# One step for both branches of the short block tiles in a sparse-attention loop, and another order around the first gated-linear-attention pair

## The chip, the cores and the metric

The kernel runs on one core of one Trainium2 chip. It is one program for a whole two-block model, launched once. The metric is device time in microseconds (us): the median of several runs of the kernel.

A core has five engines with queues of their own, each of which works strictly down its list: TensorE (PE; its weight loads are shown apart as PEld), VectorE (DVE), ScalarE (ACT), GpSimd (POOL) and SyncE (SP), which here only issues the transfers of weights. They meet through counting semaphores: `wait_ge(sem, n)` holds an engine until `sem` has reached `n`, and `then_inc(sem, 1)` counts an instruction when it is done. PE writes only into the accumulator memory `ps` (8 banks of 512 float32 columns); everything else lies in the on-chip memory, most of it in one large tensor called `arena`.

## The reference, cut to what matters

The change lies in the mixer of the second block, of which this is the core (512 tokens, width 1024):

```python
proj = h @ w_in
q_nsa, kv_nsa, g_nsa, q_gla, k_gla, v_gla, lr_gla, r_gla, g_merge = split_in_proj(proj)
...
o_a = nsa_attention(q_a, k_cmp, v_cmp, kv[2], kv[3], kv[4], kv[5], gates_a)
log_a = log_sigmoid(lr_gla @ gla_gate_w2 + gla_gate_b) / 16
o_b = gla_chunked(q_gla * 64 ** -0.5, k_gla, v_gla, log_a)     # 4 heads, keys of 64, values of 128
o_b = rmsnorm_2(o_b) * silu(r_gla)
gate_a, gate_b = split(sigmoid(g_merge), 2)
merged = gate_a * (o_a @ w_up_nsa) + gate_b * (o_b @ w_up_gla)
x = x + merged @ w_out
```

Inside `nsa_attention` each of 8 heads (64 wide, in 2 key groups) has three branches: compressed blocks, selected blocks, and a window. With 512 tokens and 16 blocks to select out of 8, the selected branch sees every earlier key, and so does the window of 512. Both are thus plain causal attention, with keys of their own (`k_slc`, `k_win`) and values of their own:

```python
p = softmax(mask(q @ k.T))          # causal
out += gate[branch] * (p @ v)       # for branch in (selected, window)
```

## The kernel before, in words

**How products are made.** Each of the large float32 products is three passes over split operands: a weight unit (128 x 1024) arrives in one of four slots of `ring`, ACT writes its upper part into `w_split` (`hi`, L1086), POOL the remainder (`lo`, L1564), and PE then does 8 x 3 matmuls of 512 columns (`unit`, L402 to L404). A split has two slots, so the split of unit n+2 waits for PE to be done with unit n. `ahead(section, k)` on ACT and on POOL is the split of the unit that comes two after (section, k) in that order. So `ahead("nsa_tm", 0)` splits the unit `kv0` and `ahead("nsa_tm", 1)` the unit `kv1`.

**The order of work** is written out by hand, one list for each engine. Nothing is scheduled by a planner; moving a line moves the instruction in that engine's queue.

**The first GLA pair.** Gated linear attention works on two pairs of heads. For pair 0, POOL makes nine products with decays (`decayed`, L1624 and L1625 for seven levels 6, 5, ... 0, each in two halves, then L1618 for the end and the state); its dictionary `between` says before which of the nine a weight split is slipped in. PE takes the scores in five groups (`pair_scores`, L855 and L866), and between these groups it works on parts of the units `kv0` and `kv1`. DVE gathers the scores level by level (`gather_pair`, L2308 and L2319) and between the levels writes the exponents of pair 1 (L1902, L1903, L1908). Then PE transposes keys (`gla_keys`, L874), runs the unit `r0`, makes the chunk states (`gla_states`, L881), half of the unit `k0`, and the outputs of head 0 (`gla_outputs`, L897 and L900). These need the chained states, which DVE writes in `chain_states` (L1938, L1942). `block_inputs(x)` (L2228, 8 small additions each) prepares the inputs of the compressed branch, which PE uses later (L820). `gate_raw(n)` (L2201) takes a finished unit `r0`, `r1`, ... for the output gate of a head.

**The NSA loop.** The selected and window branches of 8 heads run as 32 steps. A step is (p, x, tt): head pair p (one head from each key group), branch x, token tile tt of 128 queries. Tile tt sees tt + 1 blocks of 128 keys. The tiles of a pair come in the order 3, 0, 2, 1, each with both branches, one after the other. For step e:

- PE `nsa_scores`: one matmul for each of the two heads (L994)
- DVE `nsa_stats`: mask the diagonal block (L2389), negated row maximum (L2391)
- ACT `nsa_exps`: one exponential for each head, with its row sum (L1503)
- DVE `nsa_scale`: reciprocal (L2397), one scaling for each head (L2402)
- PE `nsa_transposes`: one transpose for each head and block (L1003)
- ACT `nsa_copies`: the transposed weights back out of `ps` (L1510)
- PE `nsa_values`: one matmul for each head and block (L1017)

Scores and transposes of step e use the banks 2(e % 3) and 2(e % 3) + 1, so scores of step e+2 wait for the copies of step e-1. In iteration e PE does scores(e+2), transposes(e), values(e-1), and then, where a table `GATE_AT` says so, one or three eighths of one of three units of the section `merge` in bank 7 (`gate_chunks`, L402 to L404 again). In iteration e DVE does scale(e), stats(e+2), and after the last step of a pair the additions `nsa_add` (L2411); ACT does copies(e), exps(e+2), and at fixed iterations a split of a `merge` unit or an upper part of a finished output (`outputs_hi`, L1520), whose remainder POOL then writes (L1734).

## Time and profile before

| | us |
|---|---|
| median of 3 runs | 2227.21 (2226.68 to 2233.23) |
| the profiled execution's own time | 2228.96 |
| its span (first to last instruction) | 2227.2 |
| PE busy in the span | 2159.7 (97%) |
| DVE busy | 1044.9 (47%) |
| ACT busy | 853.7 (38%) |
| POOL busy | 1173.3 (53%) |

The profile is of one execution; times in it are from the start of the span. PE is the engine that is busy nearly all the time, and the weight units that it works through make up most of that. A number of busy time alone doesn't say what bounds a stretch: for this one reads where PE sat idle and what ended each idle time. The granted clock is the share of TensorE's full speed that the chip let it have in a stretch: 1.00 is the level of 2.4 GHz, and about 0.5 the level of 1.2 GHz. The stretch of the first GLA pair lies at about 1450 to 1510 us, the NSA loop at about 1589 to 1692 us.

### The profile page before, as it was taken

The numbers are of one execution on the slowest core, as the hardware profiler recorded it, in microseconds if no ns is written. First come the engines' busy times: TensorE is split into PE (matmuls) and PEld (weight loads), VectorE is DVE, ScalarE is ACT, GpSimd is POOL, SyncE is SP. The second block draws the span as 40 slices with busy tenths as digits, with TensorE's granted clock in tenths as the row PEclk, the third lists the DMA queues.
The fourth block names the chain that finished last, engine by engine and source line by source line (L and its number), as shares of the span: only waits on it lengthen the run. The fifth ranks groups of instructions, "written<-read, shape, count | busy, mean of one in ns | idle before, by whom it ended". The sixth has DMA issues, their size and how long they took to land. (4 is left out here: it accounts for less than half of the span.)

```text
span 2227.2 us, 28340 instructions
## 1 busy us (share of the span) xinstructions
PE 2159.7 (97%) x10458; PEld 1775.8 (80%) x10458; DVE 1044.9 (47%) x1507; ACT 853.7 (38%) x1217; POOL 1173.3 (53%) x635
## 2 busy tenths in 40 slices
PE   8999999999999999899999999989989999999997
PEld 6788878888888988788888888768657888888886
DVE  7766774422433047744431436462684335422433
ACT  6565644222323234334322233434664334322222
POOL 5868755554554355435554555573213555554552
PEclk9999999999999999999999999989999999999999
DMA  4112213332332222123332332313201223332331
GB/s 166 58 57 67 65 60 94 101 105 85 95 109 80 85 88 75 56 84 101 95 106 92 95 112 78 125 49 97 74 11 58 95 95 95 95 109 89 95 108 72
DMA packets 52822, 193.30 MB, mean 87 GB/s; under 512 B 6768, under 2 KB 7680, under 8 KB 52480
## 3 DMA queue, kind: packets, MB, share of 16 engines
q1 hardware_dynamic: 50688, 184.95, 26.4%
q10 hardware_dynamic: 2048, 7.19, 0.9%
q8 instruction: 56, 0.92, 0.2%
q14 instruction: 30, 0.25, 0.0%
HBM read 187.92 MB, written 4.19 MB: 86 GB/s over the span
## 5 line engine op out<-in xcount | busy, mean ns | idle before, releaser
L1564 POOL TENSOR_TENSOR w_split<-ring,w_split 128x1024 fp32r<-128x1024 f32 (+3 forms) x327 | 842.7, 2577 | 833.6 <-ACT w_split L1086 833.6
L1086 ACT CAST w_split<-ring 128x1024 fp32r<-128x1024 f32 (+3 forms) x327 | 356.3, 1090 | 1012.2 <-PE ps L404 873.5
L402 PE MATMUL ps<-u_split,w_split 128*128 128x512 f32 x1768 | 706.9, 400 | 18.6 <-DVE u_split L1776 10.9
L404 PE MATMUL ps<-u_split,w_split 128*128 128x512 f32 x1768 | 692.7, 392 | 0.0
L403 PE MATMUL ps<-u_split,w_split 128*128 128x512 f32 x1768 | 692.1, 391 | 0.0
L402 PEld LDWEIGHTS ps<-u_split,w_split 128*128 128x128 f32 x1768 | 334.2, 189 | 96.9 <-issue 22.7
L404 PEld LDWEIGHTS ps<-u_split,w_split 128*128 128x128 f32 x1768 | 334.1, 189 | 71.0
L403 PEld LDWEIGHTS ps<-u_split,w_split 128*128 128x128 f32 x1768 | 334.3, 189 | 69.4 <-issue 3.1
L402 PE MATMUL ps<-hid,w_split 128*128 128x512 f32 x648 | 253.9, 392 | 4.2 <-DVE arena L2061 2.8
L404 PE MATMUL ps<-hid,w_split 128*128 128x512 f32 x648 | 252.9, 390 | 0.0
L403 PE MATMUL ps<-hid,w_split 128*128 128x512 f32 x648 | 252.7, 390 | 0.0
L1858 DVE TENSOR_TENSOR arena<-arena 128x512 f32<-128x512 f32 x66 | 162.0, 2454 | 66.1 <-ACT arena L1177 66.1
L1856 DVE TENSOR_TENSOR arena<-ps,rs_norm 128x512 f32<-128x512 f32 x66 | 45.7, 692 | 258.4 <-PE ps L404 236.4
L402 PEld LDWEIGHTS ps<-hid,w_split 128*128 128x128 f32 x648 | 122.1, 188 | 30.6 <-DVE arena L2061 3.2
L403 PEld LDWEIGHTS ps<-hid,w_split 128*128 128x128 f32 x648 | 122.1, 188 | 25.3 <-issue 0.2
L404 PEld LDWEIGHTS ps<-hid,w_split 128*128 128x128 f32 x648 | 121.9, 188 | 25.5
L1837 DVE TENSOR_TENSOR arena<-arena,ps 128x512 f32 x28 | 19.3, 688 | 187.5 <-PE ps L404 187.5
L1591 POOL TENSOR_TENSOR hid<-arena,hid 128x512 f32 (+1 forms) x66 | 85.2, 1292 | 5.8 <-ACT hid L1181 5.8
L1624 POOL TENSOR_TENSOR arena<-arena 128x256 f32<-128x256 f32 x70 | 63.0, 900 | 43.6 <-ACT arena L1201 43.6
L1862 DVE TENSOR_TENSOR arena<-ps,rs_norm 128x512 f32<-128x512 f32 x66 | 45.6, 691 | 81.6 <-PE ps L404 81.6
L2075 DVE TENSOR_TENSOR arena<-ps,mixer_consts 64x512 f32<-64x512 f32 x48 | 33.1, 689 | 88.1 <-ACT arena L1325 86.9
L1201 ACT ACTIVATE arena<-arena 128x1024 f32<-128x1024 f32 (+2 forms) x40 | 42.0, 1059 | 64.9 <-DVE arena L1903 61.7
(312 smaller groups left out, 2606.1 us busy)
## 6 DMA issues: line engine op xcount, KB each, us to landing
ring<-in_w_hgrn SPq DMA_DIRECT2D x32, 512.0 KB, 3.5
ring<-in_w_attn_qk SPq DMA_DIRECT2D x24, 512.0 KB, 3.5
ring<-in_w_merge SPq DMA_DIRECT2D x24, 512.0 KB, 3.3
ring<-in_w_gu0a SPq DMA_DIRECT2D x22, 512.0 KB, 3.5
ring<-in_w_gu0b SPq DMA_DIRECT2D x22, 512.0 KB, 3.5
ring<-in_w_gu1a SPq DMA_DIRECT2D x22, 512.0 KB, 3.6
ring<-in_w_gu1b SPq DMA_DIRECT2D x22, 512.0 KB, 3.5
ring<-in_w_gu2a SPq DMA_DIRECT2D x22, 512.0 KB, 3.5
```

What stands on the lines that cost most here:

```text
L402: nc.tensor.matmul(ps[:, bank], ws[:, 0, r, w], act[:, 0, c], start=c == 0, stop=False)
L403: nc.tensor.matmul(ps[:, bank], ws[:, 0, r, w], act[:, 1, c], start=False, stop=False)
L404: m = nc.tensor.matmul(ps[:, bank], ws[:, 1, r, w], act[:, 0, c], start=False, stop=c == n - 1)
L1086: nc.scalar.copy(ws[:, 0, slot, 0:w], ring[:, r, 0:w]).then_inc(s["w_hi"], 1)
L1201: nc.scalar.activation(dv[:, lo:hi], dv[:, lo:hi], ACT.Exp).then_inc(s["dec_out"], 1)
L1564: nc.gpsimd.tensor_tensor(ws[:, 1, slot, 0:w], ring[:, r, 0:w], ws[:, 0, slot, 0:w].bitcast(F32), ALU.subtract).then_inc(s["w_lo"], 1)
L1591: nc.gpsimd.tensor_tensor(dst, gtmp[:, j % 2], src.bitcast(F32), ALU.subtract).then_inc(s["g_lo"], 1)
L1624: nc.gpsimd.tensor_tensor(x[:, :, 0], x[:, :, 0], kk[:, :, 0], ALU.mult)
L1856: nc.vector.tensor_tensor(gnorm[:, x], ps[:, 2 * x], rs[:], ALU.mult).then_inc(s["gate_norm"], 1)
L1858: nc.vector.tensor_tensor(sgate[:, x], sgate[:, x], gnorm[:, x], ALU.mult).then_inc(s["gate_silu"], 1)
L1862: nc.vector.tensor_tensor(gtmp[:, x], ps[:, 2 * x + 1], rs[:], ALU.mult).then_inc(s["up_norm"], 1)
L2075: nc.vector.tensor_tensor(tsin[dst, N % 2], ps[src, N % 4], sin_a[src], ALU.mult).then_inc(s["rope_sin"], 1)
```

## The change

It has two parts.

**Around the first GLA pair.** On POOL the split of `kv0` comes before the third level product instead of the fifth, and the split of `kv1` before the seventh (level 0) instead of the eighth. On DVE `block_inputs(0)` comes behind `gate_raw(0)` and `chain_states`, and `block_inputs(1)` behind `gla_gated(0)` and `gate_raw(1)`.

**In the NSA loop.** The tiles with one block (tt = 0) and two blocks (tt = 1) are done for both branches in one step, so that a pair of heads has 6 steps instead of 8 and the loop 24 instead of 32. The tiles of a pair now come in the order 3, 0, 2, 1 as before, as the steps: 3 first branch, 3 second branch, 0 both, 2 first, 2 second, 1 both. In a step with both branches one mask, one maximum, one reciprocal and one copy serve both; scores, exponentials, scalings, transposes and value products are as many as before in all. The 24 eighths of `merge` units stand in 17 places instead of 22, some of two eighths; the ACT lines that are tied to an iteration number are shifted to match.

The diff, cut to its core:

```diff
-        nneg, nsum, nrec = [take(3, 2) for _ in range(3)]
+        nneg, nsum, nrec = [take(3, 4) for _ in range(3)]
...
-        GATE_AT = {0: (0, 0, 3)}
-        GATE_AT.update({e: (0, e + 2, e + 3) for e in range(1, 6)})
...
+        GATE_AT = {0: (0, 0, 3), 1: (0, 3, 4), 2: (0, 4, 6), 3: (0, 6, 7), 4: (0, 7, 8),
...
+        GATE_END = {4: 0, 12: 1, 20: 2}
...
-        STEPS = [(p, x, tt) for p in range(HEADS_N // 2) for tt in (3, 0, 2, 1) for x in range(2)]
+        TILE_STEPS = ((3, (0,)), (3, (1,)), (0, (0, 1)), (2, (0,)), (2, (1,)), (1, (0, 1)))
+        PER_PAIR = len(TILE_STEPS)
+        STEPS = [(p, xs, tt) for p in range(HEADS_N // 2) for tt, xs in TILE_STEPS]
+        ROWS_DONE = [2 * sum(len(xs) for _, xs, _ in STEPS[:e]) for e in range(len(STEPS) + 1)]
...
+        def step_blocks(e):
+            _, xs, tt = STEPS[e]
+            return len(xs) * (tt + 1)
+
+        def by_branch(e, v):
+
+            return v.rearrange("p h (x n) -> p h x n", x=len(STEPS[e][1]))
...
             def nsa_scores(e):
...
+                for i, x in enumerate(xs):
+                    for k, hh in enumerate(PAIR[p]):
+                        rows = slice(k * HD, k * HD + HD)
+                        m = nc.tensor.matmul(by_branch(e, step_banks(e, step_blocks(e)))[:, k, i],
+                                             q_n[rows, hh % 4, tt * P:(tt + 1) * P],
+                                             k_n[rows, x, 0:(tt + 1) * P], start=True, stop=True)
                 m.then_inc(s["ns_ps"], 1)
             def nsa_transposes(e):
...
+                for i in range(len(xs)):
+                    for k in range(2):
+                        pe.wait_ge(s["ns_scaled"], ROWS_DONE[e] + 2 * i + k + 1)
...
             def nsa_exps(e):
+                n = step_blocks(e)
                 act.wait_ge(s["ns_neg"], e + 1)
+                for i in range(len(STEPS[e][1])):
+                    for k in range(2):
+                        row = slice(k * len(STEPS[e][1]) + i, k * len(STEPS[e][1]) + i + 1)
+                        nc.scalar.activation(by_branch(e, prob[:, e % 3, :, 0:n * P])[:, k, i],
...
             for e in range(len(STEPS)):
                 nsa_copies(e)
...
-                if 5 <= e < 5 + HEADS_G:
-                    outputs_hi(e - 5)
+                if 4 <= e < 4 + HEADS_G:
+                    outputs_hi(e - 4)
...
-                if e in (20, 22):
-                    outputs_hi(HEADS_G + (e - 20) // 2)
+                if e in (15, 17):
+                    outputs_hi(HEADS_G + (e - 15) // 2)
...
-            decayed(HEADS_H, gdec, kg[:, 0], qg[:, 0], between={4: lambda: ahead("nsa_tm", 0), 7: lambda: ahead("nsa_tm", 1)})
+            decayed(HEADS_H, gdec, kg[:, 0], qg[:, 0], between={2: lambda: ahead("nsa_tm", 0), 6: lambda: ahead("nsa_tm", 1)})
...
             end_exponents(la[:, 1], gdec)
-            block_inputs(0)
             gate_raw(0)
             chain_states(HEADS_H, HEADS_H, gst, gchd[:, 0])
+            block_inputs(0)
             gla_silu(0)
-            block_inputs(1)
             gla_scaled(0)
             gla_gated(0)
             gate_raw(1)
+            block_inputs(1)
             gla_silu(1)
...
             def nsa_stats(e):
-                n = STEPS[e][2] + 1
+                _, xs, tt = STEPS[e]
+                rows = by_branch(e, step_banks(e, step_blocks(e)))
                 dve.wait_ge(s["ns_ps"], e + 1)
...
             def nsa_scale(e):
...
-                dve.wait_ge(s["ns_exp"], 2 * e + 2)
...
+                dve.wait_ge(s["ns_exp"], ROWS_DONE[e + 1])
...
-                dve.wait_ge(s["no_ps"], 8 * (p + 1))
+                dve.wait_ge(s["no_ps"], PER_PAIR * (p + 1))
```

**POOL, the first GLA pair.** Level products are the rows with three numbers (128x16x16 is level 4, 128x256 level 0); `w_split<-ring,w_split` is a split, first of `kv0`, then of `kv1`. Before, from level 4 on:

```order
L1624 TENSOR_TENSOR arena<-arena 128x16x16
L1625 TENSOR_TENSOR arena<-arena 128x16x16
L1624 TENSOR_TENSOR arena<-arena 128x32x8
L1625 TENSOR_TENSOR arena<-arena 128x32x8
L1564 TENSOR_TENSOR w_split<-ring,w_split 128x1024
L1624 TENSOR_TENSOR arena<-arena 128x64x4
L1625 TENSOR_TENSOR arena<-arena 128x64x4
L1624 TENSOR_TENSOR arena<-arena 128x128x2
L1625 TENSOR_TENSOR arena<-arena 128x128x2
L1624 TENSOR_TENSOR arena<-arena 128x256
L1625 TENSOR_TENSOR arena<-arena 128x256
L1564 TENSOR_TENSOR w_split<-ring,w_split 128x1024
```

The same place of the changed kernel, from level 5 on (its L1643, L1644 and L1583 are L1624, L1625 and L1564 of before):

```order
L1643 TENSOR_TENSOR arena<-arena 128x8x32
L1644 TENSOR_TENSOR arena<-arena 128x8x32
L1583 TENSOR_TENSOR w_split<-ring,w_split 128x1024
L1643 TENSOR_TENSOR arena<-arena 128x16x16
L1644 TENSOR_TENSOR arena<-arena 128x16x16
L1643 TENSOR_TENSOR arena<-arena 128x32x8
L1644 TENSOR_TENSOR arena<-arena 128x32x8
L1643 TENSOR_TENSOR arena<-arena 128x64x4
L1644 TENSOR_TENSOR arena<-arena 128x64x4
L1643 TENSOR_TENSOR arena<-arena 128x128x2
L1644 TENSOR_TENSOR arena<-arena 128x128x2
L1583 TENSOR_TENSOR w_split<-ring,w_split 128x1024
```

The split of `kv0` has moved ahead of the four products of levels 4 and 3, and that of `kv1` ahead of the two of level 0.

**DVE, after the gathering of the first pair.** L1908 is the last exponent of pair 1; `x8` with `64x8x31` is `block_inputs`. Before:

```order
L1908 TENSOR_TENSOR arena<-arena 128x512
L2228 TENSOR_TENSOR arena<-arena,mixer_consts 64x8x31 x8
L2201 TENSOR_TENSOR arena<-ps,rs_norm 128x512
L1938 COPY arena<-ps 128x128
L1942 SCALAR_TENSOR_TENSOR arena<-arena,ps 128x128 x2
L2282 TENSOR_TENSOR arena<-arena 128x512
L2228 TENSOR_TENSOR arena<-arena,mixer_consts 64x8x31 x8
L2287 SCALAR_TENSOR_TENSOR arena<-ps,small,arena 128x512
L2293 TENSOR_TENSOR arena<-arena 128x512
L2201 TENSOR_TENSOR arena<-ps,rs_norm 128x512
```

The same place of the changed kernel:

```order
L1927 TENSOR_TENSOR arena<-arena 128x512
L2220 TENSOR_TENSOR arena<-ps,rs_norm 128x512
L1957 COPY arena<-ps 128x128
L1961 SCALAR_TENSOR_TENSOR arena<-arena,ps 128x128 x2
L2247 TENSOR_TENSOR arena<-arena,mixer_consts 64x8x31 x8
L2301 TENSOR_TENSOR arena<-arena 128x512
L2306 SCALAR_TENSOR_TENSOR arena<-ps,small,arena 128x512
L2312 TENSOR_TENSOR arena<-arena 128x512
L2220 TENSOR_TENSOR arena<-ps,rs_norm 128x512
L2247 TENSOR_TENSOR arena<-arena,mixer_consts 64x8x31 x8
```

`gate_raw(0)` and the three instructions of `chain_states` now stand ahead of both groups of eight.

**PE, an early iteration of the NSA loop.** In a row `128x384 x2` are scores, `ident_sb` transposes, `64x128` value products, `u_split` an eighth of a `merge` unit. Before, iterations 2 and 3 (tile 0, first and second branch):

```order
L994 MATMUL ps<-arena 128x384 x2
L1003 MATMUL ps<-ident_sb,arena 128x128 x2
L1017 MATMUL ps<-arena 64x128 x8
L402 MATMUL ps<-u_split,w_split 128x512
L403 MATMUL ps<-u_split,w_split 128x512
L404 MATMUL ps<-u_split,w_split 128x512
L994 MATMUL ps<-arena 128x384 x2
L1003 MATMUL ps<-ident_sb,arena 128x128 x2
L1017 MATMUL ps<-arena 64x128 x2
```

The changed kernel, iteration 2 (tile 0, both branches) and the scores of the next:

```order
L1005 MATMUL ps<-arena 128x384 x2
L1017 MATMUL ps<-ident_sb,arena 128x128 x4
L1033 MATMUL ps<-arena 64x128 x8
L412 MATMUL ps<-u_split,w_split 128x512
L413 MATMUL ps<-u_split,w_split 128x512
L414 MATMUL ps<-u_split,w_split 128x512
L412 MATMUL ps<-u_split,w_split 128x512
L413 MATMUL ps<-u_split,w_split 128x512
L414 MATMUL ps<-u_split,w_split 128x512
L1005 MATMUL ps<-arena 128x256 x4
```

Two groups of two transposes have become one of four, and two places of one eighth one place of two.

## Rows read from the trace of the kernel before

**Rows 1.** PE's waits from 1453 to 1588.7 us: total us, times, longest.

```profile
PE ps L897 <- DVE arena L1942: 5.9, 1, 5.9
PE ps L402 <- POOL w_split L1564: 2.6, 1, 2.6
```

**Rows 2.** Busy us by stretch: PE, PEld, DVE, ACT, POOL; clock, DMA share, GB/s.

```profile
1457.50:1461.30 3.80, 3.78 (x9) 2.57 (x9) 0.00 (x0) 0.97 (x4) 3.80 (x6) 0.55 0.00 0
1487.50:1493.40 5.90, 0.01 (x1) 0.00 (x0) 5.74 (x10) 1.11 (x2) 5.47 (x6) 0.88 0.00 0
1493.40:1502.30 8.90, 8.84 (x27) 7.28 (x28) 4.50 (x9) 2.03 (x3) 0.00 (x0) 0.50 0.01 2
1588.70:1692.20 103.50, 92.39 (x682) 56.33 (x680) 80.78 (x174) 62.74 (x170) 17.44 (x11) 0.98 0.10 37
1669.70:1673.00 3.30, 3.25 (x17) 2.59 (x18) 1.40 (x4) 1.25 (x3) 0.00 (x0) 0.51 0.02 5
```

**Rows 3.** PE's waits in the NSA loop, 1588.7 to 1692.3 us.

```profile
PE ps L1003 <- DVE arena L2402: 5.9, 9, 1.9
PE ps L994 <- ACT arena L1510: 4.1, 4, 1.5
PE ps L402 <- POOL w_split L1564: 0.7, 1, 0.7
```

**Rows 4.** PE's timeline, first GLA pair: start, us, what.

```profile
1453.76 1.16 PE L855 MATMUL ps<-arena 64*128 64x128 f32 x16
...
1463.25 0.50 PE L402 MATMUL ps<-u_split,w_split 128*128 128x512 f32 x1
...
1466.90 2.00 PE L866 MATMUL ps<-arena 64*128 64x64 f32 x32
```

**Rows 5.** POOL's timeline, first GLA pair.

```profile
1452.27 0.73 POOL L1624 TENSOR_TENSOR arena<-arena 128x256 f32<-128x256 f32 x1
...
1455.02 2.35 POOL L1564 TENSOR_TENSOR w_split<-ring,w_split 128x1024 fp32r<-128x1024 f32 x1
```

**Rows 6.** DVE's timeline, first GLA pair.

```profile
1464.76 2.32 DVE L1902 TENSOR_TENSOR arena<-arena 128x256 f32<-128x256 f32 x1
...
1482.55 8.96 DVE L2228 TENSOR_TENSOR arena<-arena,mixer_consts 64x248 f32<-64x248 f32 x8
...
1492.47 0.73 DVE L1942 SCALAR_TENSOR_TENSOR arena<-arena,ps 128x128 f32<-128x128 f32 x2
...
1493.72 4.28 DVE L2228 TENSOR_TENSOR arena<-arena,mixer_consts 64x248 f32<-64x248 f32 x8
1508.00 0.75 DVE L2287 SCALAR_TENSOR_TENSOR arena<-ps,small,arena 128x512 f32<-128x512 f32 x1 [10.00 <-ACT arena L1219]
```

**Rows 7.** PE's timeline in the NSA loop, a piece without waits.

```profile
1628.80 0.92 PE L994 MATMUL ps<-arena 64*128 64x384 f32 x4
1629.65 0.44 PE L1003 MATMUL ps<-ident_sb,arena 128*128 128x128 f32 x2
1630.02 0.44 PE L1017 MATMUL ps<-arena 128*64 128x128 f32 x4
1630.39 0.50 PE L402 MATMUL ps<-u_split,w_split 128*128 128x512 f32 x1
...
1631.28 0.70 PE L994 MATMUL ps<-arena 64*128 64x256 f32 x4
1631.92 0.87 PE L1003 MATMUL ps<-ident_sb,arena 128*128 128x128 f32 x6
1632.72 0.44 PE L1017 MATMUL ps<-arena 128*64 128x128 f32 x4
```

**Rows 8.** Groups by shape in the NSA loop: busy us, mean ns, idle before.

```profile
L2391 DVE TENSOR_REDUCE arena<-ps 128x2 f32<-128x1024 f32 x8 | 9.8, 1225 | 0.3
...
L1503 ACT ACTIVATE arena<-ps,arena 128x256 f32<-128x256 f32 x16 | 7.5, 478 | 0.0
...
L2402 DVE TENSOR_SCALAR arena<-arena 128x256 f32<-128x256 f32 x16 | 6.0, 419 | 0.3
```

More of the change, by code:

```diff
@@ L980, in nsa_scores @@
             def nsa_scores(e):
-                p, x, tt = STEPS[e]
+                p, xs, tt = STEPS[e]
                 if e == 0:
@@ L1012, in nsa_values @@
                     pe.wait_ge(s["oa_acc"], 2 * p)
-                for b in range(tt + 1):
-                    for k, hh in enumerate(PAIR[p]):
-                        vcols = slice(x * P + k * HD, x * P + k * HD + HD)
-                        rows = slice(hh % 2 * HD, hh % 2 * HD + HD)
-                        m = nc.tensor.matmul(ps[rows, 6, tt * P:(tt + 1) * P], vsw[:, b, vcols],
-                                             probT[:, e % 2, k, b * P:(b + 1) * P],
-                                             start=x == 0 and b == 0, stop=x == 1 and b == tt)
+                for i, x in enumerate(xs):
+                    for b in range(tt + 1):
+                        at = i * (tt + 1) + b
+                        for k, hh in enumerate(PAIR[p]):
+                            vcols = slice(x * P + k * HD, x * P + k * HD + HD)
+                            rows = slice(hh % 2 * HD, hh % 2 * HD + HD)
+                            m = nc.tensor.matmul(ps[rows, 6, tt * P:(tt + 1) * P], vsw[:, b, vcols],
+                                                 probT[:, e % 2, k, at * P:(at + 1) * P],
+                                                 start=x == 0 and b == 0, stop=x == 1 and b == tt)
                 m.then_inc(s["no_ps"], 1)
@@ L2430, in _ @@
                     add_sin(e + 2)
-                if e % 8 == 0 and e:
-                    nsa_add(e // 8 - 1)
+                if e % PER_PAIR == 0 and e:
+                    nsa_add(e // PER_PAIR - 1)
                 if e - 1 in GATE_END:
```

58 lines of the change are left out of this document (27 added, 31 removed).

## The prediction

> **What bounds the kernel now.** I first looked for PE's idle time, since PE is busy almost everywhere and a microsecond is worth something only where PE would otherwise stand still. The view of waits, for the stretch that holds the GLA and the preparation of NSA, shows two long ones [rows 1]: 5.9 us at the first output matmul (L897), ended by DVE's chained states (L1942), and 2.6 us at the first matmul of the unit `kv0` (L402), ended by POOL's split. The third in that stretch is 0.3 us. So after 1496 us PE is fed without a break up to 1589 us, and what is won before is not waited away there unless something else is late.
>
> Second, the granted clock [rows 2]. After the 2.6 us wait the stretch 1457.5 to 1461.3 ran at 0.55, after the 5.9 us wait 1493.4 to 1502.3 ran at 0.50: the level of 1.2 GHz, each time right after PE had stood idle. Inside the NSA loop 1669.7 to 1673.0 ran at 0.51, after a wait of 1.9 us, the longest there [rows 3]. A long wait is paid twice.
>
> Third, the NSA loop, 103.5 us, of which PE is busy 92.4 [rows 2]: 11.1 us idle, made up of 5.9 for scaled weights, 4.1 for banks that ACT had not copied out, and 0.7 for a split [rows 3]; the rest is small. DVE is busy 80.8 and ACT 62.7 us of the same 103.5, so PE has the most work, and DVE is not far behind.
>
> **First GLA pair, POOL.** PE was done with the diagonal scores at 1453.76 + 1.16 = 1454.92 [rows 4]; POOL began to split `kv0` at 1455.02 and took 2.35 us [rows 5], hence the wait. Now the split comes two levels earlier, where level 4 began: at 1452.27 [rows 5], which gives 1452.27 + 2.35 = 1454.62, before PE asks. ACT's upper part is long there. The 2.6 us go. With them the low clock goes: nine matmuls filled the 3.80 us [rows 2]; at full clock 15 matmuls fill 1466.90 - 1463.25 = 3.65 us, start to start of what follows [rows 4], which is 0.24 each, so nine take 2.2 to 2.3. That returns 1.5 us. What is pushed back on POOL is levels 4 and 3, by 2.35 us, to about 1457.4. PE needs them after the rest of `kv0`, at some 1462.5: hidden. The split of `kv1`, moved ahead of level 0, then ends at about 1463, PE wants it at about 1464.5, and level 0 follows by 1464.5 for scores that come at 1472: hidden.
>
> **First GLA pair, DVE.** Before, eight additions of `block_inputs(0)` stood from 1482.55 for 8.96 us in front of `gate_raw(0)` and the chained states, which ended at 1492.47 + 0.73 = 1493.20 [rows 6]; PE went on at once. Nobody asks for those additions until some 20 us later. Now the states come straight after `gate_raw(0)`. PE ends the half of `k0` at 1487.5, where the idle stretch begins [rows 2], and the chunk states twelve matmuls before it, 12 x 0.24 = 2.9 us; the chained states, a copy and two updates of which the updates take 0.73 [rows 6], are done some 1.3 us after the chunk states, and PE does not wait. 5.9 us go. The low clock after it held for 8.9 us at 0.50 [rows 2], a loss of at most 4.4 us; part of the time of small matmuls does not scale with the clock, and I take 4.0.
>
> What is late next: the additions now run beside head 0's outputs, and `gla_silu(0)` and `gla_scaled(0)` stand behind them. DVE waited 10.0 us for the root of `gla_scaled(0)`, after the second group of eight (4.28 us), which now comes later [rows 6]: 14.3 us of room, less the 6 us by which PE's outputs move up towards it, so the first group would at 4.28 us fit easily and at its slow 8.96 us just about. The second group falls into the wait for a sigmoid. I cost both at nothing; without cover it would be up to 2 us.
>
> A rule that speaks against this order: the Trainium skill, "SBUF — State Buffer", section "Who interferes with whom", says that a DVE operation with two inputs in this memory and a GpSimd operation that reads it exclude each other, for the whole instruction. The trace has its price: a DVE level product took 2.32 us at 1464.76, with POOL at work, and the eight additions 8.96 against 4.28 us [rows 6]. With the split of `kv1` earlier, it meets DVE's first exponents of pair 1. One instruction of up to 2.3 us more could stand ahead of DVE's levels; PE then has matmuls of `kv1` left as cover, so I take 0 and keep 2.3 as a bound.
>
> Sum here: 2.6 + 1.5 + 5.9 + 4.0 = 14.0 us. Bounds: 6 us (idle time only, 8.5, less 2.3) and 15 us.
>
> **NSA loop, fewer groups.** PE pays for each change of a group. In a piece without waits [rows 7] scores of 384 columns take 1629.65 - 1628.80 = 0.85 and of 256 columns 1631.92 - 1631.28 = 0.64: 0.21 for 128 columns, 0.22 fixed. Two transposes take 0.37, six 0.80: 0.11 each, 0.15 fixed. Value products I take as alike, 0.15. An eighth of a `merge` unit takes 1631.28 - 1630.39 = 0.89; three matmuls in a row are 3 x 0.23 (the 3.65 us of [rows 4] less such a start, by 15), so 0.20 fixed. Eight steps fewer save 8 x (0.22 + 0.15 + 0.15) = 4.2 us, five places fewer for eighths 5 x 0.20 = 1.0. Together 5.2 us. If the fixed part of scores belongs to each matmul and not to the group, it is 3.4.
>
> **NSA loop, waits.** Now 10.8 us by name [rows 3] and 3.3 x 0.49 = 1.6 us of clock [rows 2], 12.4 in all. Unchanged stay the fill of the first steps (about 1.8 us: three steps of latency with nothing behind them) and most of what happens at the change of head pair, where no eighths are left to cover the additions on DVE and the ACT queue holds a split and an upper part. Less: 24 steps instead of 32 in which a latency can show, and DVE saves a mask, a maximum's start and a reciprocal eight times (0.5 us each). More: a step with both branches is a longer chain. For two blocks: maximum 1.23, four exponentials at 0.48, four scalings at 0.42 [rows 8], with the mask and the reciprocal in all about 5.7 us. In the middle of the loop two iterations of 3.6 us lie over it. At the end nothing does: the last step is such a one, and I estimate 2 us more there. From 12.4 I take off the half of what is neither fill nor tail (about 4 us) and add 2: 10.5. So the waits give 2, and the loop 7 us in all. Bounds: the merged chain adds a microsecond to each of the eight merged steps and nothing else improves: 5.2 - 8 = -3; all waits but fill and tail go: 5.2 + 7 = 12.
>
> **The sum.** 14.0 + 7.0 = 21.0 us less. Against the profiled execution's 2228.96 (span 2227.2, 1.8 around it) that is 2208.0; the median of the runs is 2227.21, 1.75 lower, so the forecast is 2206.2 us. What follows, the products of `merge`, `mix_out` and the last feed-forward, is bound by PE and moves forward as it is; its weights are asked for as PE frees slots.
>
> **Rivals.**
> *A. The clock or another wait takes half of the GLA part.* DVE's own list for this pair is dense; when PE is 4 us earlier, DVE must be too, and if blocked instructions keep it from that, PE waits a little at the outputs and may stay at 1.2 GHz. For it: 0.50 after such a wait, and the 2.32 us instruction [rows 2, 6]. Against: DVE works in answer to PE's scores and so starts earlier as well. GLA gives 7: 2227.2 - 14 = 2213 us.
> *B. The loop gives nothing.* The longer chains and the last step eat the 5.2 us. For it: DVE's 80.8 of 103.5 us, and no eighths in 7 of 24 iterations. Against: the middle of the loop without waits. 2227.2 - 14 = 2213 us.
> *C. The loop gives all.* 12 us: 2201.
> *D. The moves miss.* If `gate_raw(0)`, which waits for the unit `r0`, is late, the states are no earlier; the additions were only beside the real cause. Against it: `gate_raw(0)` and the chained states (1.3 us later) follow the eight additions, which end at 1491.51, without a break [rows 6]. Only the loop and 4 us of `kv0` are left: 2227.2 - 11 = 2216.
> *E. Slower.* Three pairs of banks go round: scores of step e+2 wait for the copies of step e-1. If a two-block step holds its banks for scores, 5.7 us, transposes and copy, 8.7 us in all, and the in-order queues let no more than one other step run beside it, a step costs 4.4 us on the mean and the loop 104; if the order of waits lets them run almost singly, the loop grows. From 124 us for the loop (5.2 us a step) it eats the GLA gain and the rest and the kernel is slower; at 130 us it would be 2227.2 - 14 + 26.5 = 2240.
>
> **Numbers.** My forecast 0.57, A 0.16, B 0.14, C 0.06, D 0.04, E 0.03. About 0.3% (6.7 us) is what a measurement can tell from no change here. Only E is slower: 0.03; within 0.3% lie E's mild forms and D at its worst: 0.03; faster 0.94. The range takes in A, B, D's middle and C: 2199 to 2216 us.
>
> **What would show it.** In the profile after: PE's waits for L1942's and the `kv0` split's successors gone, the granted clock 1.00 from 1454 to 1500 us; first scores of the NSA loop at about 1574.7 instead of 1588.75. The loop about 96 us long, PE busy in it a few us less, waits of some 10 us, with one of over a microsecond before the last transposes. Wrong is the first part if PE waits more than 1 us at head 0's outputs; the second if the loop takes over 101 or under 92 us.

## The result, and the profile after

| | before | changed | ratio, 95% interval |
|---|---|---|---|
| median of 11 runs each, on the same chips, us | 2231.89 | 2219.16 | 0.9948 [0.9938, 0.9958] |
| lowest and highest, us | 2226.68 to 2234.33 | 2211.10 to 2221.38 | |
| profiled execution, us | 2228.96 | 2218.95 | |

The change makes the kernel faster by 0.52%, some 11.6 us of 2227.21, where 21.0 were forecast. The measured 2219.16 us lies outside 2199 to 2216. Part of that distance is the base: the median of before was 2227.21 in its first three runs and 2231.89 in eleven. The gain itself is what fell short.

PE's waits in the profile of the changed kernel, first up to the NSA loop, then in it (engine, line, what it waited for: us in total, times, longest):

```profile
PE ps L876 <- DVE arena L2338: 4.9, 1, 4.9
PE ps L626 <- POOL w_split L1583: 1.0, 1, 1.0
...
PE ps L1017 <- DVE arena L2425: 5.3, 7, 1.9
PE ps L1005 <- ACT arena L1529: 1.4, 2, 1.1
PE ps L412 <- POOL w_split L1583: 0.5, 1, 0.5
PE ps L1033 <- ACT arena L1529: 0.3, 1, 0.3
```

Both waits of [rows 1] are gone. The 1.0 us at L626 lies before the first GLA pair, and before had it too. A new wait stands in the pair: the third group of level matmuls (L876) waits 4.9 us for the masked copies of the second (L2338, DVE), which free its bank.

The same stretches as in [rows 2] by windows (stretch, its length, busy us and count of PE, PEld, DVE, ACT, POOL, PE's granted clock, DMA):

```profile
1457.50:1461.30 3.80, 3.80 (x41) 3.39 (x42) 1.90 (x9) 1.20 (x5) 3.80 (x6) 1.00 0.00 0
1472.70:1481.50 8.80, 8.72 (x44) 7.32 (x44) 6.11 (x16) 1.06 (x1) 2.26 (x3) 0.52 0.01 2
1492.40:1502.30 9.90, 9.90 (x48) 7.87 (x47) 9.77 (x9) 6.88 (x9) 9.69 (x8) 1.00 0.15 53
1556.00:1559.70 3.70, 3.70 (x60) 3.70 (x61) 0.00 (x0) 0.00 (x0) 0.00 (x0) 0.99 0.00 0
1559.70:1570.40 10.70, 10.70 (x37) 8.88 (x36) 4.96 (x5) 4.22 (x4) 0.00 (x0) 0.52 0.01 2
1587.60:1682.30 94.70, 87.06 (x682) 56.98 (x681) 74.91 (x150) 61.25 (x162) 17.52 (x11) 0.98 0.12 40
```

The clock is full where it was half in [rows 2], and half in two other places: after the new wait, and from 1559.7 us, where PE had not stood idle at all. There it had just done 60 of the 64 matmuls of the compressed scores (L852, 32 columns each; "the short matmuls" from here on), in 3.70 us.

Six starts in PE's timeline place what was gained and lost (start, us, what, and the idle time before it in brackets):

```profile
1462.90 2.00 PE L876 MATMUL ps<-arena 64*128 64x64 f32 x32
1472.78 3.68 PE L876 MATMUL ps<-arena 64*128 64x64 f32 x32 [4.93 <-DVE arena L2338]
1481.54 1.11 PE L876 MATMUL ps<-arena 64*128 64x64 f32 x16
1492.20 1.05 PE L907 MATMUL ps<-arena 128*128 128x128 f32 x8
1555.90 4.85 PE L852 MATMUL ps<-arena 64*128 64x32 f32 x64
1587.62 2.43 PE L1005 MATMUL ps<-arena 64*128 64x512 f32 x16
```

Before, the third and fourth level groups and the short matmuls started at:

```profile
1471.78 2.00 PE L866 MATMUL ps<-arena 64*128 64x64 f32 x32
1476.68 1.11 PE L866 MATMUL ps<-arena 64*128 64x64 f32 x16
...
1561.28 4.39 PE L842 MATMUL ps<-arena 64*128 64x32 f32 x64
```

The second level group starts at 1462.90 in place of 1466.90 [rows 4]: 4.0 us ahead. The third starts 1.0 us behind before's, after the new wait, and the fourth 4.9 behind, after the half clock. Head 0's outputs (L907) start at 1492.20, without a wait, in place of 1493.4 [rows 2]: only 1.2 ahead, and with the low clock behind them gone 5.2. The short matmuls start 5.4 ahead. From there to the NSA loop PE needed 31.7 us in place of 27.5: 4.2 lost to the half clock. The NSA loop starts at 1587.62 in place of 1588.75: 1.1 ahead. It ends at 1682.29 in place of 1692.31, 10.0 ahead, and that is the whole of 2228.96 - 2218.95: nothing behind the loop changed. So the GLA part gave 1.1 us where 14.0 were forecast, the loop 8.9 where 7.0 were.

Why L2338 was late: DVE (three rows), POOL (six) and ACT (two) in the changed kernel.

```profile
1460.45 0.44 DVE L2338 COPY_PREDICATED arena<-lvl_mask_sb,ps 128x256 f32<-128x256 uint32 x1
1460.79 8.87 DVE L1921 TENSOR_TENSOR arena<-arena 128x256 f32<-128x256 f32 x1
1469.58 0.41 DVE L1922 TENSOR_TENSOR arena<-arena 128x256 f32<-128x256 f32 x1
...
1460.56 2.39 POOL L1583 TENSOR_TENSOR w_split<-ring,w_split 128x1024 fp32r<-128x1024 f32 x1
1462.91 0.84 POOL L1643 TENSOR_TENSOR arena<-arena 128x256 f32<-128x256 f32 x1
1463.71 0.85 POOL L1644 TENSOR_TENSOR arena<-arena 128x256 f32<-128x256 f32 x1
1464.51 2.56 POOL L1637 TENSOR_TENSOR arena<-arena 128x512 f32<-128x512 f32 x2
1466.99 2.38 POOL L1583 TENSOR_TENSOR w_split<-ring,w_split 128x1024 fp32r<-128x1024 f32 x1
1471.83 0.73 POOL L1643 TENSOR_TENSOR arena<-arena 128x256 f32<-128x256 f32 x1 [2.45 <-ACT arena L1217]
...
1463.01 1.05 ACT L1102 CAST w_split<-ring 128x1024 fp32r<-128x1024 f32 x1 [4.31 <-PE ps L414]
1470.70 1.06 ACT L1217 ACTIVATE arena<-arena 128x1024 f32<-128x1024 f32 x1 [5.34 <-DVE arena L1922]
```

DVE's first exponent for pair 1 (L1921) is recorded over 8.87 us; its twin takes 0.41. It ends at 1469.66, 0.29 us after POOL's run (1466.99 + 2.38 = 1469.37). POOL had worked without a gap through the split of `kv1`, the last level products, two other products and the split of `r0`. The second masked copies stand behind that exponent in DVE's queue, and PE's third level group behind them.

Before, the same exponent (L1902 there) took 2.32 us from 1464.76 [rows 6], beside these two rows of POOL:

```profile
1464.21 2.58 POOL L1618 TENSOR_TENSOR arena<-arena 128x512 f32<-128x512 f32 x2
1468.13 2.39 POOL L1564 TENSOR_TENSOR w_split<-ring,w_split 128x1024 fp32r<-128x1024 f32 x1 [1.33 <-ACT w_split L1086]
```

It began in the first of the two products and ended at 1467.08, 0.29 us after the second (1464.21 + 2.58 = 1466.79), in a pause in which POOL waited 1.33 us for ACT.

### The profile page after: what moved, and what is told of

The parts are those of the page before. It is cut to its first block and busy times, and to the rows that moved or that the text cites. A ratio compares the mean times of both kernels' runs of the same rounds, so it can differ in the third digit from the quotient of the medians.

```text
span 2217.1 us, 28302 instructions
## 1 busy us (share of the span) xinstructions
PE 2157.2 (97%) x10458; PEld 1779.5 (80%) x10458; DVE 1050.2 (47%) x1483; ACT 852.3 (38%) x1209; POOL 1173.3 (53%) x635
## 5 line engine op out<-in xcount | busy, mean ns | idle before, releaser
L1583 POOL TENSOR_TENSOR w_split<-ring,w_split 128x1024 fp32r<-128x1024 f32 (+3 forms) x327 | 842.8, 2578 | 825.9 <-ACT w_split L1102 825.8
L412 PE MATMUL ps<-u_split,w_split 128*128 128x512 f32 x1768 | 707.4, 400 | 15.6 <-DVE u_split L1795 10.7
L412 PEld LDWEIGHTS ps<-u_split,w_split 128*128 128x128 f32 x1768 | 334.6, 189 | 93.2 <-issue 18.7
L1643 POOL TENSOR_TENSOR arena<-arena 128x256 f32<-128x256 f32 x70 | 62.9, 898 | 46.1 <-ACT arena L1217 46.1
```

Of the source, the lines that this page charges most:

```text
L412: nc.tensor.matmul(ps[:, bank], ws[:, 0, r, w], act[:, 0, c], start=c == 0, stop=False)
L1583: nc.gpsimd.tensor_tensor(ws[:, 1, slot, 0:w], ring[:, r, 0:w], ws[:, 0, slot, 0:w].bitcast(F32), ALU.subtract).then_inc(s["w_lo"], 1)
L1643: nc.gpsimd.tensor_tensor(x[:, :, 0], x[:, :, 0], kk[:, :, 0], ALU.mult)
```

## Experiments

Each kernel ran on a chip beside before. Ratios are to before on that chip, whose medians there were 2229.9 to 2232.9 us. Theory: DVE's two-input instruction is kept out while POOL's instructions follow each other without a pause, and that new wait with the half clock behind it took 8.8 us of the gain; the half clock behind the short matmuls took the rest. The runs bear this out in part: steps28, below, shows that the exclusion does not always last as long as POOL's run.

**nsa_only**: the changed kernel with POOL's and DVE's order of before.

```diff
-            decayed(HEADS_H, gdec, kg[:, 0], qg[:, 0], between={2: lambda: ahead("nsa_tm", 0), 6: lambda: ahead("nsa_tm", 1)})
+            decayed(HEADS_H, gdec, kg[:, 0], qg[:, 0], between={4: lambda: ahead("nsa_tm", 0), 7: lambda: ahead("nsa_tm", 1)})
...
+            block_inputs(0)
             gate_raw(0)
             chain_states(HEADS_H, HEADS_H, gst, gchd[:, 0])
-            block_inputs(0)
             gla_silu(0)
+            block_inputs(1)
...
-            block_inputs(1)
```

> The changed kernel without its moves around the first GLA pair: only the NSA loop of 24 steps. The loop took 94.6 us in the changed kernel and 103.5 before (first scores to first product of the merge), so this should be 9 us faster than before; the two PE waits of 5.9 and 2.6 us and the low clock behind them stay as before. If the loop's gain hung on the moves (another alignment of POOL's splits), it would be 5 us or less.

Measured: 2221.75 us, 0.9967 [0.9955, 0.9978]: 7.4 us by the ratio, between the 9 and the 5 of the two expectations. Its loop took 95.9 us (1595.43 to 1691.31), in place of 103.6.

One thing went otherwise than expected. The program up to the loop is that of before, and after the 2.6 us wait at `kv0` the clock stayed at 1.00 in this profile. With PE that much earlier, POOL's pause was gone here too, and the exponent stood for 6.24 us, until 0.28 us after the end of POOL's run. DVE, POOL, PE:

```profile
1464.16 6.24 DVE L1921 TENSOR_TENSOR arena<-arena 128x256 f32<-128x256 f32 x1
...
1467.71 2.41 POOL L1583 TENSOR_TENSOR w_split<-ring,w_split 128x1024 fp32r<-128x1024 f32 x1
...
1473.53 2.79 PE L876 MATMUL ps<-arena 64*128 64x64 f32 x32 [2.31 <-DVE arena L2338]
```

So before's own order can run into the new wait. The profiled execution was the longest of its seven (2228.31 us, granted clock over the whole span, "mean clock" below, 0.988; the other six 2221.08 to 2225.89, 0.990 or 0.991), so it doesn't stand for the median.

**gla_only**: the reverse, before with the new order of POOL and DVE alone (32 steps).

> The kernel before with only the moves on POOL and DVE around the first GLA pair. Theory 1 (DVE's first exponent of pair 1 starves behind a run of POOL instructions without a pause, which comes about as soon as PE is 4 us earlier): 4.1 + 9.9 - 8.8 = 5 us faster than before, with a PE wait of about 5 us at the third group of level scores. Theory 2 (the low clock after the short matmuls of the compressed scores, 1560 to 1570 us in the changed kernel, is a lasting result of the moves and not chance): 5 - 5 = no gain. My estimate is 5 us by theory 1, and the low clock after the compressed scores in some executions only.

Measured: 2226.35 us, 0.9986 [0.9975, 0.9997]. That is 3.1 us by the ratio, between the 5 of theory 1 and the nothing of theory 2. Its profile has the new wait (5.0 us at L866, an exponent of 8.89 us) and the half clock behind the short matmuls. The two halves give 0.33% and 0.14%: the loop made most of the gain, the GLA moves hardly any.

**pool_back**: the changed kernel with POOL's two splits back in their old places; DVE's moves and the 24 steps stay.

```diff
-            decayed(HEADS_H, gdec, kg[:, 0], qg[:, 0], between={2: lambda: ahead("nsa_tm", 0), 6: lambda: ahead("nsa_tm", 1)})
+            decayed(HEADS_H, gdec, kg[:, 0], qg[:, 0], between={4: lambda: ahead("nsa_tm", 0), 7: lambda: ahead("nsa_tm", 1)})
```

> The changed kernel with the two POOL splits back where they were (before the fifth and the eighth product); DVE's moves and the 24 steps stay. Theory 1: the 2.6 us wait for the kv0 split and its low clock come back (4.1 us), but the 4.9 us wait at the third group and its low clock (8.8 us in all) go, because POOL pauses while DVE wants its exponents: 4.7 us faster than the changed kernel, 19 us faster than before less the clock chance. Rival (the DVE wait comes from DVE's own order): the 4.9 us wait stays and the kernel is 4 us slower than the changed one.

Measured: 2211.73 us, 0.9917 [0.9904, 0.9930]: 7.4 us less than the changed kernel (6.9 by the ratios), where 4.7 were expected. The earlier splits cost more than the 2.6 us wait and its clock that they save. POOL and DVE in its profile (2214.92 us, the longest of its five; short matmuls at 1550.12, 5.8 us ahead of the changed kernel's):

```profile
1463.34 2.55 POOL L1637 TENSOR_TENSOR arena<-arena 128x512 f32<-128x512 f32 x2
1467.20 2.40 POOL L1583 TENSOR_TENSOR w_split<-ring,w_split 128x1024 fp32r<-128x1024 f32 x1 [1.30 <-ACT w_split L1102]
...
1463.85 2.33 DVE L1921 TENSOR_TENSOR arena<-arena 128x256 f32<-128x256 f32 x1
1466.10 0.41 DVE L1922 TENSOR_TENSOR arena<-arena 128x256 f32<-128x256 f32 x1
```

POOL waits 1.30 us for ACT's upper part of `r0`, and there DVE's exponent gets through, after 2.33 us. ACT writes that part when PE is done with the unit before (1466.07, against 1463.01 in the changed kernel), and PE, held up at `kv0`, was late with it. Taking PE's wait away, with the half clock behind it, took POOL's pause away.

**kv1_back**: only the split of `kv1` back to its old place ({2, 7}).

> The changed kernel with only the kv1 split back behind level 0 (kv0's split stays before the third product). Theory 1 (any run of POOL instructions without a pause keeps DVE out; the run is as long whatever stands where in it): DVE's first exponent still takes about 9 us and PE waits about 5 us, time as the changed kernel. Theory 3 (it is the split of kv1, one long instruction, that keeps DVE out): the exponent comes through after level 0, at 2 us or less, and the kernel is 5 to 9 us faster than the changed one.

Measured: 2219.03 us, 0.9949 [0.9937, 0.9962]; wait 5.0 us, exponent 8.93 us. Where `kv1` stands doesn't matter: the exponent again ended with POOL's run, 0.27 us behind it.

**r0_later**: the changed kernel with the split of `r0` behind the first of pair 1's level products.

```diff
-            mid("kv0")
             decayed(HEADS_H + 1, gdec, kg[:, 1], qg[:, 1],
-                    between={2: lambda: mid("kv1"), 4: lambda: mid("r0"), 7: lambda: mid("k0"), 8: lambda: mid("r1")})
+                    between={1: lambda: mid("kv0"), 2: lambda: mid("kv1"), 4: lambda: mid("r0"), 7: lambda: mid("k0"), 8: lambda: mid("r1")})
```

(`mid("kv0")` on POOL issues the next unit's split, that of `r0`.)

> The changed kernel, with POOL's split of r0 taken from in front of pair 1's levels and put behind the first of its level products, so that POOL's run from the split of kv1 to the last level product of pair 0 is followed by a product that reads other data, and the split comes later. Theory (DVE's first exponent of pair 1 is kept out as long as POOL's instructions follow each other without a pause): the pause of POOL comes some 2.3 us earlier if the level product has to wait for DVE's exponents; the exponent then ends at about 1467.3 instead of 1469.7 us, PE's wait at the level matmuls falls from 4.9 to about 2.6 us, and the time is 2 to 6 us under the changed kernel's 2219 us. Rival (the exponent is late for another reason, in DVE's own list): wait still 4.9 us, time within 1 us of 2219.

Measured: 2215.58 us, 0.9926 [0.9912, 0.9939]; PE's wait 2.6 us as expected. The exponent began at 1462.35 and took 6.54 us, to 1468.89; POOL's run ended at 1468.62. (POOL's run began 1.5 us later here, so its end is not at 1467.)

**exps_later**: the changed kernel with DVE's exponents for levels 6 and 5 one group later.

```diff
-                for l in {1: (6, 5), 2: (4, 3), 3: (2, 1), 4: (0,)}.get(n, ()):
+                for l in {2: (6, 5, 4, 3), 3: (2, 1), 4: (0,)}.get(n, ()):
```

> The changed kernel, with DVE's exponents for levels 6 and 5 of the next pair computed one group later than now. So DVE first does its level products of pair 0 and meets POOL's run with nothing that PE asks for soon. Theory (the loss at the first pair is the position of this one blocked instruction in DVE's list): PE's wait of 4.9 us before the level matmuls is gone, and the 3.9 us of half clock after it too; a wait of up to 2 us may stand a group later; time about 2212 us, 5 to 8 us under the changed kernel. Rival (POOL's run keeps out whichever two-input instruction DVE has next): the level product itself is blocked, the wait moves but stays near 5 us, time within 1.5 us of 2219.

Measured: 2211.91 us, 0.9912 [0.9898, 0.9926]: 7.2 us less than the changed kernel (8.0 by the ratios), as expected. Its short matmuls start at 1548.55, 12.7 us ahead of before's, near the 14.0 that the forecast had for this part. The exponent now meets the tail of POOL's run (3.36 us at 1466.37, again ending with it) and PE waits 1.4 us. The product that moved ahead of it (L2214) took 0.69 us in the middle of POOL's run, so the rival is out: it is not every two-input instruction of DVE that is kept out. L2214 takes one input from PSUM, the exponent both from SBUF.

**scores_split**: the changed kernel with the 64 short matmuls in two halves.

```diff
...
-            compressed_scores()
+            compressed_scores((0, 1))
+            mid("r2", (3, 6))
+            compressed_scores((2, 3))
             gla_outputs(2)
-            mid("r2", (3, 8))
+            mid("r2", (6, 8))
```

> The changed kernel, with PE's 64 short matmuls of the compressed scores in two halves of 32 and three parts of the unit r2 between them; nothing is added or left out. Theory (the granted clock falls behind the 64 matmuls of 32 columns because PE counts as little used during them, and 10.7 us at 0.52 after them cost some 4.7 us): with large matmuls between, the clock stays at 1.00 there and the time is 3 to 5 us under 2219. Rival (the clock falls there for another reason, or the low stretch costs nothing because PE then waits for DVE and ACT at the NSA loop's start): within 1 us of 2219.

Measured: 2219.35 us, 0.9943 [0.9930, 0.9957]. A miss: the half clock still came, behind the second half.

**both**: exps_later and scores_split together.

> The changed kernel with both edits: exponents of levels 6 and 5 a group later, and the compressed scores in two halves. Theory: the two losses are in different places and their gains add: 5 to 8 us and 3 to 5 us, so 2206 to 2211 us, which is the forecast's 2206.2 at best. Rival (both are cover for one thing, the start of the NSA loop, which waits for DVE and ACT): no more than the better of the two alone.

Measured: 2210.89 us, 0.9907 [0.9892, 0.9923], within the noise of exps_later alone: the gains did not add.

**scores_quarter**: exps_later with 16 short matmuls instead of 64; the other 48 are left out, and the compressed branch reads old values there.

```diff
-                for tt in range(TT):
+                for tt in range(TT - 1, TT):
```

> The kernel of exps_later with 48 of the 64 short matmuls of the compressed scores left out (those of three of the four row tiles), so the compressed branch reads old values there. It takes 3.6 us of PE away by itself. Theory (the short matmuls bring the clock down, and that costs about 4.4 us): the half clock behind them is gone and the first scores of the NSA loop come 3.6 + 4.4 = 8 us earlier, unless DVE and ACT are not ready for the loop; time 2204 to 2207. Rival (something else brings it down): half clock still there, 3.6 us or less gained, time about 2208 to 2211.

Measured: 2203.56 us, 0.9877 [0.9861, 0.9892]. The stretch behind them, by windows, in scores_quarter and in exps_later:

```profile
1549.40:1559.40 10.00, 10.00 (x45) 7.35 (x45) 7.13 (x8) 6.65 (x7) 2.54 (x2) 1.00 0.17 52
```
```profile
1548.60:1553.40 4.80, 4.80 (x66) 4.74 (x65) 0.00 (x0) 0.00 (x0) 0.00 (x0) 0.88 0.00 0
1553.40:1562.60 9.20, 9.20 (x29) 7.55 (x29) 4.96 (x5) 4.22 (x4) 0.00 (x0) 0.51 0.01 2
```

Its short matmuls begin at 1547.90 and fill 1.5 us, where the 64 fill 4.3 at full clock (1561.28 to 1565.60 in before); the 48 are thus 2.8 us of work, less than the 3.6 expected. From the first of them to the loop it took 24.6 us (to 1572.52) in place of 31.7 (1548.55 to 1580.24), 7.1 less. Without the 2.8 of work that leaves 4.2 for the half clock, as in the comparison with before. The time went down by 8.35 (7.8 by the ratios). With those 2.8 us of work put back this kernel would stand at some 2206.4, beside the forecast's 2206.2.

**scores_moved**: exps_later with the short matmuls behind the outputs of head 2 and the rest of `r2`.

> The kernel of exps_later with PE's 64 short matmuls of the compressed scores moved whole behind the rest of the unit r2: first the outputs of head 2, then five eighths of r2, then the short matmuls. Theory (the short matmuls bring the clock down): the stretch at half clock moves with them, beginning about 5 us later against r2, and the time is within 1.5 us of exps_later's 2211.9. Rival (the outputs of head 2 and the 64-partition matmuls beside them bring it down, or it is a matter of when the clock last rose): the half clock stays where it is against the program, before the rest of r2, or is gone, and in that case the time is 3 to 5 us less.

Measured: 2214.99 us, 0.9933 [0.9919, 0.9946]. Neither expectation held. The clock stayed at 1.00 behind the short ones (1555 to 1565 us), but DVE had the compressed scores 5 us later, and PE then waited 3.7 us for DVE's L2306 at head 3's outputs (L2306 itself had waited 2.3 us for ACT), with half clock behind that. One loss for another.

**outputs_apart**: exps_later with three eighths of `r2` between the short matmuls and head 2's outputs.

```diff
             compressed_scores()
+            mid("r2", (3, 6))
             gla_outputs(2)
-            mid("r2", (3, 8))
+            mid("r2", (6, 8))
```

> The kernel of exps_later with three eighths of the unit r2 (nine matmuls of 512 columns) put between the 64 short matmuls and the outputs of head 2, so that large matmuls follow the short ones, as in scores_moved, while the scores come as early as in exps_later. Theory (short matmuls followed by the small ones of the outputs bring the clock down): 1.00 behind them, first scores of the NSA loop at about 1576 instead of 1580.2, time about 2208. Rival (what follows doesn't matter): about half clock over some 9 us behind them as in exps_later, time 2211 to 2213.

Measured: 2210.75 us, 0.9915 [0.9901, 0.9928]. Half clock behind the short ones again (0.52 from 1550 to 1555 us), as the rival had it: large matmuls right behind them don't prevent it.

**before_again, before_third, after_again**: the two kernels once more, one profile each.

> The kernel before, unchanged, profiled a second time. Theory (whether the clock falls behind the short matmuls of the compressed scores differs from execution to execution of one kernel, and the first profile of before was one without it): the same stretch now runs at about half clock, and the time is up to 5 us over 2228.96. Rival (before's order keeps the clock up there, and the change is what brings it down): 1.00 there again, and the same waits of 2.6 and 5.9 us.

> The kernel before, profiled a third time. If executions of one kernel differ in the clock behind the short matmuls, half clock there now and then, with a time above 2231 us; if before's order keeps the clock up, 1.00 again.

> The changed kernel, profiled a second time. Either as in its first profile (exponent of 8.9 us, wait 4.9 us, about 2219 us), or, if the exclusion of DVE by POOL is a matter of the moment at which they meet, as in the profile of steps28 (exponent of 2.5 us, wait 0.9 us, 2211 to 2214 us); in both half clock behind the short matmuls.

Measured: 2229.25, 2230.78 and 2218.78 us. Both profiles of before have 1.00 behind the short matmuls, as the first has; after_again repeats the first profile of the change (exponent 8.90, wait 5.0, 0.50 there). So neither profile bears my theory for before_again out.

They don't refute it either. Of the 47 other executions of before beside the experiments, 17 had a mean clock of 0.988 and took 2231.9 to 2234.3 us; 15 had 0.992, and all but one of these took 2226.1 to 2228.7. The three profiled ones had 0.990 or 0.991, so none was of the first kind. As an estimate, 10.7 us at 0.52 lower the mean over 2217 us by 0.002: enough for about half of that difference. Which stretch was low in those 17 their times can't show.

**steps28**: the changed kernel with only the one-block tile merged, 28 steps.

```diff
...
-        TILE_STEPS = ((3, (0,)), (3, (1,)), (0, (0, 1)), (2, (0,)), (2, (1,)), (1, (0, 1)))
+        TILE_STEPS = ((3, (0,)), (3, (1,)), (0, (0, 1)), (2, (0,)), (2, (1,)), (1, (0,)), (1, (1,)))
...
```

> The changed kernel with only the one-block tile merged: both branches of two blocks are steps of their own again, 28 steps in place of 24, the eighths of the merge units spread over 20 of them. Theory (the gain of the loop is made of a fixed price for each step: 0.52 us of fixed parts and as much again of waits, in all some 1.1 us a step): the NSA loop takes about 94.6 + 4.4 = 99 us, the time is about 2223.5. Rival 1 (the long chain of a two-block step gives back what it saves): the loop stays at 94 to 96 us, time 2217 to 2220. Rival 2 (the two-block steps made nearly all of the gain, since the one-block steps were too short to matter): the loop takes 102 us or more, time over 2226.

Measured: 2219.60 us, 0.9949 [0.9936, 0.9962]. Its loop took 96.5 us, all at full clock:

```profile
1581.30:1677.80 96.50, 88.46 (x682) 55.44 (x681) 78.16 (x162) 61.77 (x166) 17.38 (x10) 1.00 0.11 39
```

Comparable at full clock: before 103.56 less 1.6 for its low stretch, 102.0; r0_later's 24 steps, at 1.00 too, 93.2. Merging the four one-block tiles gave 5.5 us, the four two-block tiles 3.3; 4.4 each was expected, so a fixed price for each step is not borne out. The time lies in rival 1's 2217 to 2220, its loop just above rival 1's 96. The median doesn't show these 3.3 us, since the intervals of both kernels are that wide.

Its profiled execution took 2214.48 us, the other four 2218.51 to 2220.04, and up to the loop its program is that of the changed kernel. DVE in it, and the third level group on PE:

```profile
1460.71 2.47 DVE L1921 TENSOR_TENSOR arena<-arena 128x256 f32<-128x256 f32 x1
1463.11 1.07 DVE L1922 TENSOR_TENSOR arena<-arena 128x256 f32<-128x256 f32 x1
1464.10 1.06 DVE L1921 TENSOR_TENSOR arena<-arena 128x256 f32<-128x256 f32 x1
1465.08 1.51 DVE L1922 TENSOR_TENSOR arena<-arena 128x256 f32<-128x256 f32 x1
...
1468.72 2.00 PE L876 MATMUL ps<-arena 64*128 64x64 f32 x32 [0.94 <-DVE arena L2338]
```

Here the exponent was kept out for one split only, and then DVE and POOL took turns: DVE's at 1.06 us in place of 0.41, POOL's at 1.05 in place of 0.84. The wait was 0.9 us instead of 4.9, and the loop began 6.35 us earlier than in the changed kernel's profile. So the exclusion is not certain: two of the changed kernel's own eleven executions, 2211.10 and 2212.79 us, may be of this kind, or have kept the clock up behind the short matmuls, which their times alone can't show.

The changed kernel's own profile says the same 14 us after the long exponent, where POOL again works without a pause. DVE, POOL:

```profile
1483.83 1.63 DVE L1921 TENSOR_TENSOR arena<-arena 128x256 f32<-128x256 f32 x1
...
1482.77 2.41 POOL L1583 TENSOR_TENSOR w_split<-ring,w_split 128x1024 fp32r<-128x1024 f32 x1 [7.81 <-ACT w_split L1102]
1485.13 0.92 POOL L1643 TENSOR_TENSOR arena<-arena 128x256 f32<-128x256 f32 x1
```

This exponent ended at 1485.46, 0.28 us after the split and not after the run. In all these rows a pause of POOL let DVE in, and sometimes the end of one instruction was enough. What decides between the two no run here shows.

## Why the prediction was wrong

The direction was right, and so were the two parts as places of gain; the size was not: 11.6 us by ratio against 21.0. The loop gave more than forecast, the GLA part next to nothing.

- *`kv0`, 2.6 + 1.5.* Right: 4.0 us ahead at 1462.90, clock 1.00.
- *States, 5.9 + 4.0.* Right: L907 without a wait, 1.00 behind it. What was feared behind them didn't come: `block_inputs(0)` took 10.7 us beside POOL, slower than its slow 8.96, and `gla_scaled(0)` (1502.67) was just in time for PE at 1503.46. The prediction's own sign for this part, a wait at head 0's outputs, thus stayed silent; its other one, full clock from 1454 to 1500 us, did not (0.52 at 1472.7 to 1481.5).
- *"One instruction of up to 2.3 us more could stand ahead of DVE's levels ... so I take 0 and keep 2.3 as a bound."* This is the step that failed. The instruction took 8.87 us. I read the price off one instance [rows 6], as that of being kept out for one instruction of POOL's. Before's rows (above, POOL at 1464.21) show that it spanned the rest of one POOL instruction and all of the next, up to POOL's pause. And L1902 is no level product, as the prediction calls it, but the very exponent that the change then held up. At this place the price was how long POOL went on without a pause, and the change both brought the exponent forward and removed the pause. PE's cover was not enough: a wait of 4.9 us, and by the prediction's own measure (4.0 lost in 8.9 us at 0.50) 3.9 in the 8.8 us at 0.52; the fourth level group, from 1.0 to 4.9 us behind before's, shows the same 3.9. Together 8.8 of the 12.9 us that the GLA part fell short; pool_back and exps_later got 7.4 and 7.2 back. The bound for the sum, 6 us, counted one such blocked instruction and no clock behind a new wait. Rival A had the mechanism (blocked DVE instructions, a wait, half clock), but put the wait at the outputs and the loss at 7, where 12.9 were missing; its chance was 0.16. The Trainium skill, "SBUF — State Buffer", section "Who interferes with whom", was the right place to look: the runs agree that DVE is kept out (8.87 us in place of 0.41), and show that this can outlast the one instruction that it speaks of.
- *Clock at 1.00 up to the loop.* Wrong from 1559.7 us. Another 4.2 us went there, by the starts above and by scores_quarter. The first profile of before showed 1.00 at that place, so nothing in it warned of this.
- *Loop, fewer groups: 5.2.* PE's busy time fell by 92.39 - 87.06 = 5.3 us.
- *Loop, waits: 2.* By name 10.7 before, 7.5 now: 3.2. The wait forecast ahead of the last transposes did not come: the 1.9 us stand ahead of the last but one (1677.25), and before had as long a wait at 1669.75. The ones for ACT's copies went, from 4.1 to 1.4, which I had not foreseen. The loop took 94.7, forecast about 96.

The gain that was not there is accounted for: 14.0 - 8.8 - 4.2 = 1.0, against 1.1 measured.

Open: why the clock falls behind the short matmuls in all twelve profiles that hold all 64 of them ahead of head 2's outputs and have a part of the change, and in none of three of before. That the change causes it is not shown: nsa_only has before's program up to the loop and shows it too, and none of before's executions with a mean clock of 0.988 was profiled. Large matmuls behind them (outputs_apart) or between two halves (scores_split) don't prevent it. In the one profile with 16 of them the clock stayed up, and in the one with all 64 behind the outputs (scores_moved) as well; what tips it is open. Open too is why an exponent is sometimes let in between two POOL instructions and sometimes not.

exps_later, pool_back, both and outputs_apart (2210.8 to 2211.9 us) beat both kernels, and can't be told from each other.

## What to carry to other kernels

Before a stall is removed, look at what other engines do in its shadow. POOL's short wait here was a consequence of PE's wait and of the half clock behind it, and it was the gap through which DVE got at its data; whoever closes one closes the other. When the price of a blocked instruction is read from one row, look at the other engine's rows beside it: how many instructions it spans, and what ended it. Where DVE works on SBUF alone beside POOL, count POOL's run up to its next pause as the worst case of one DVE instruction, and keep the DVE instruction on which PE waits next ahead of such a run or behind it. And profile more than one execution, with their mean clocks beside the median's, before a stretch of low clock is laid to a change. Take the saving of idle time as provisional until the clock in the new trace has been read: it can be paid out again at a place where PE never waits.

## What the runs showed of the hardware that was not expected

- One DVE instruction (128x256, two inputs in SBUF, 0.41 us alone) was recorded over 8.87 to 8.93 us in the changed kernel (both profiles), gla_only and kv1_back. In these, and over 6.54 us in r0_later, 6.24 in nsa_only, 3.36 in exps_later and 2.32 in before, it ended 0.27 to 0.29 us after the last instruction of POOL's run. One with an input from PSUM took 0.69 us in such a run.
- In another execution with the same program up to there they took turns: 1.06 and 1.07 us for DVE's, 1.05 and 1.02 us for POOL's. In the changed kernel a later one was let in 0.28 us after one POOL instruction (1485.46), with the next already recorded from 1485.13.
- PE's clock went to half without any idle time, behind 64 matmuls of 32 columns that filled 4.85 us, for 10.7 us in the changed kernel and 9.2 in exps_later; not in three profiles of before with the same 64, nor behind 16 of them.
- After the 2.6 us wait at `kv0` the clock fell in the three profiles of before (0.55) and stayed up in that of nsa_only (1.00): the same wait doesn't always cost the same.
